# Fourier mixer on folded time with half the transform, its panels first; the products of the state-space tables one step behind their transposes

## The reference

```
ff = f.reshape(1, 1024, 4 heads, 64)
mixed = fft2(ff, axes=(time, channel of the head), norm='ortho').real
y_fft = einsum('bshd,hde->bshe', mixed, w_fft)
```

## Time and profile before

| | us |
|---|---|
| three runs | 2754.02, 2754.80, 2760.42 |
| median | 2754.8 |
| span of the profiled execution, first to last instruction | 2751.9 |
| median less that span | 2.9 |
| PE busy | 2637.7 |
| DVE, POOL, ACT busy | 1465.6, 1091.4, 1029.3 |
| mean granted clock of TensorE | 0.986 |

### The profile page before, as it was taken

How to read it: one execution, slowest core, us unless ns; L and a number is a source line. 1 busy time by engine, 2 the same in 40 slices (tenths; PEclk the granted TensorE clock), 3 DMA queues, 4 the chain that set the end, 5 groups by cost and what they waited for, 6 DMA issues and landing times.

```text
span 2751.9 us, 31627 instructions
## 1 busy us (share of the span) xinstructions
PE 2637.7 (96%) x12542; PEld 2080.4 (76%) x12542; DVE 1465.6 (53%) x1881; ACT 1029.3 (37%) x1600; POOL 1091.4 (40%) x605
## 2 busy tenths in 40 slices
PE   6889989999999999999999999999999999999997
PEld 2657757777888788877777788888788788888885
DVE  5646658797777722276766422433457655322225
ACT  4413655455444511345454321211354434312112
POOL 1322114256656544442211142322353655534443
PEclk8999999999999999999999999999999999999998
DMA  6453247321222343241123122111324233433322
GB/s 247 178 146 101 78 173 285 113 81 66 81 84 83 112 146 126 84 145 59 54 68 109 54 88 67 58 48 48 137 91 153 77 115 104 149 118 128 115 77 85
DMA packets 109619, 297.92 MB, mean 108 GB/s; under 512 B 13344, under 2 KB 28192, under 8 KB 109472
## 3 DMA queue, kind: packets, MB, share of 16 engines
q1 hardware_dynamic: 102592, 275.36, 29.4%
q10 hardware_dynamic: 3456, 10.73, 1.0%
q0 software_dynamic: 3424, 9.81, 0.9%
HBM read 233.09 MB, written 62.76 MB: 108 GB/s over the span
## 4 chain that ended last, share of the span: by engine, by line
PE 71%; DVE 5%; ACT 1%; issue 1%; POOL 1%; DMA 1%; POOLq 0%; SPq 0%; DVEq 0%; ACTq 0%
PE ps L1698 16%; PE ps L1700 15%; PE ps L1699 15%; PE ps L1732 5%; PE ps L1734 5%; PE ps L1733 5%; PE pc L1732 1%; PE pc L1734 1%; PE pc L1733 1%; PE pss L2026 1%; PE pc L2078 1%; PE pc L2080 1%; PE pc L2079 1%; POOL whl L3448 1%; DVE pad L2104 0%
## 5 line engine op out<-in xcount | busy, mean ns | idle before, releaser
L3448 POOL TENSOR_TENSOR whl<-wraw,whl 128x1024 fp32r<-128x1024 f32 (+2 forms) x309 | 648.0, 2102 | 1242.0 <-ACT whl L2918 1241.8
L1698 PE MATMUL ps<-act,whl 128*128 128x512 f32 x1824 | 735.5, 403 | 34.7 <-DVE act L2098 9.2
L1699 PE MATMUL ps<-act,whl 128*128 128x512 f32 x1824 | 718.0, 394 | 0.0
L1700 PE MATMUL ps<-act,whl 128*128 128x512 f32 x1824 | 717.5, 393 | 0.0
L1698 PEld LDWEIGHTS ps<-act,whl 128*128 128x128 f32 x1824 | 344.9, 189 | 134.9 <-issue 43.3
L2918 ACT ACTIVATE whl<-wraw 128x1024 fp32r<-128x1024 f32 (+2 forms) x309 | 268.1, 869 | 461.9 <-PE ps L1700 372.6
L1700 PEld LDWEIGHTS ps<-act,whl 128*128 128x128 f32 x1824 | 344.9, 189 | 76.9
L1699 PEld LDWEIGHTS ps<-act,whl 128*128 128x128 f32 x1824 | 345.3, 189 | 75.7 <-issue 4.1
L2098 DVE TENSOR_TENSOR y<-y,ps 128x512 f32<-128x512 f32 x176 | 120.9, 687 | 365.6 <-PE ps L1700 365.4
L1698 PE MATMUL ps<-hid,whl 128*128 128x512 f32 x544 | 216.8, 399 | 4.4 <-DVE y L2502 4.3
L1700 PE MATMUL ps<-hid,whl 128*128 128x512 f32 x544 | 214.4, 394 | 0.0
(11 more groups left out here) (402 smaller groups left out, 4206.1 us busy)
## 6 DMA issues: line engine op xcount, KB each, us to landing
wraw<-in_w_in SPq DMA_DIRECT2D x63, 512.0 KB, 3.4
wraw<-in_f1u SPq DMA_DIRECT2D x72, 256.0 KB, 2.8
wraw<-in_f2d SPq DMA_DIRECT2D x36, 512.0 KB, 3.4
wraw<-in_w_out SPq DMA_DIRECT2D x32, 512.0 KB, 3.4
x<-in_w_ada SPq DMA_DIRECT2D x32, 512.0 KB, 7.2
hid<-hscr SPq DMA_DIRECT2D x29, 512.0 KB, 6.6
xs<-y SPq DMA_DIRECT2D x24, 512.0 KB, 6.3
wraw<-in_f2u SPq DMA_DIRECT2D x48, 256.0 KB, 3.3
```

The lines of the kernel that those rows point to most:

```text
L1698: pe.matmul(PSB[g.bank][:, :], hi, x_hi, start=e == 0, stop=False)
L1699: pe.matmul(PSB[g.bank][:, :], hi, x_lo, start=False, stop=False)
L1700: m = pe.matmul(PSB[g.bank][:, :], lo, x_hi, start=False, stop=e == len(ks) - 1)
L3448: return g_.tensor_tensor(out, a, b, op)
```

## The change

Time is folded: for t = 1 to 511, e(t) = f(t) + f(1024-t) goes to a new tile `fe` and f(t) - f(1024-t) stays in fT (`fft_eo` on DVE); the cosine half needs e alone, the sine half the difference alone. So `fft_c` and `fft_s` run over 4 time tiles in place of 8; f(512) is carried separately (`fft_n`, two products of one column) and added with alternating sign in `fft_out`. All four `dft` panels are loaded once. Panels 8 and 9 come first in w_in; `fft_w` goes behind panel 1 on a bank half of `pss`, the stage behind panel 2. In `tables`, `tab_ko` moves from the step of its `tab_k` one or two steps on, and the thread has one step more.

```diff
-W_IN_ORDER = (0, 1, 2, 8, 9, 6, 7, 3, 4, 5)
+W_IN_ORDER = (8, 9, 0, 1, 2, 6, 7, 3, 4, 5)
...
-        def made_k(b0):
+        def turn_k(b0):
             p.put("tab_k", b0)
             p.put("tab_wst", b0)
+
+        def made_k(b0):
             p.put("tab_ko", b0)
             p.put("tab_kst", b0)
...
             if n:
-                made_k(b0 - GB)
+                turn_k(b0 - GB)
             yield
             p.put("tab_w", b0)
+            if n > 5:
+                made_k(b0 - GB)
             yield
             if n < 6:
                 p.put("tab_cs", n)
                 p.put("tab_cst", n)
+                if n:
+                    made_k(b0 - GB)
                 yield
+        turn_k(NG - GB)
+        yield
         made_k(NG - GB)
...
     def fourier():
-        p.put("fft_w", p.hold[0])
-        for tp in range(8):
-            p.pe(0.9, "fft_c", tp, p.hold[1])
+        for tp in range(4):
+            p.pe(0.9, "fft_c", tp, p.hold[0], p.hold[1])
             p.poll()
-        for tp in range(8):
+        p.pe(0.5, "fft_n")
+        for tp in range(4):
             p.pe(3.4, "fft_s", tp, p.hold[2], p.hold[3])
             p.poll()
-        p.pe(3.4, "fft_mid")
+        p.pe(1.8, "fft_mid")
...
-                if r[0] == 0:
-                    p.put("fft_load")
-            if r[0] == 9:
-                fourier()
+                if r[0] == 1:
+                    p.pe(1.8, "fft_w")
+                elif r[0] == 2:
+                    fourier()
+            if r[0] == 8:
+                p.put("fft_load")
+            if r[0] in (8, 9):
+                p.put("fft_eo", r[0] - 8)
...
                 if b < 5:
                     w.wait_ge(*done("ssmD", "rot", b + 1))
+                else:
+                    w.wait_ge(*done("ssmA", "y", 4))
...
                 for pr in range(2):
-                    w.wait_ge(*z_done(8 + pr))
-                    m = pe.matmul(PSB[tp % 2][:, pr * 256:pr * 256 + 256], fT[:, pr, tp * 128:tp * 128 + 128],
-                                  WC[:, pr, :, :].rearrange("p a b -> p (a b)"), start=True, stop=True)
+                    w.wait_ge(*done("fftD", "eo", pr))
+                    for i, part in enumerate((fe, fT)):
+                        q = pr * 256 + i * 128
+                        m = pe.matmul(PSB[tp % 2][:, q:q + 128], part[:, pr, c], WC[:, pr, i, :], start=True, stop=True)
...
+            def fft_n():
+                for pr in range(2):
+                    m = pe.matmul(PSS[:, 0, 2 + pr:3 + pr], WC[:, pr, 0, :], fT[:, pr, 512:513], start=True, stop=True)
...
                     for pr in range(2):
                         m = pe.matmul(PSB[2 * i + pr][:, :], FA[tp][:, pr, i * 128:i * 128 + 128],
-                                      dft[tp % 4][:, i * 512:i * 512 + 512], start=tp == 0, stop=tp == 7)
+                                      dft[tp][:, i * 512:i * 512 + 512], start=tp == 0, stop=tp == 3)
...
+            def fft_eo(pr):
+                f, back, e = fT[:, pr, 1:512], fT[:, pr, 1023:512:-1], fe[:, pr, :]
+                w.wait_ge(*z_done(8 + pr))
+                v.tensor_copy(e[:, 0:1], fT[:, pr, 0:1]).then_inc(*step("fftD"))
+                tt(e[:, 1:512], f, back, ALU.add).then_inc(*step("fftD"))
+                w.wait_ge(*last("fftD"))
+                tt(f, f, back, ALU.subtract).then_inc(*mark("fftD", "eo", pr))
...
-                v.tensor_copy(st[:, 0:512], Pb[:, :]).then_inc(*mark("fftD", "a", pr))
+                ts(st[:, 0:512:2], Pb[:, 0:512:2], n512, ALU.add).then_inc(*step("fftD"))
+                ts(st[:, 1:512:2], Pb[:, 1:512:2], n512, ALU.subtract).then_inc(*mark("fftD", "a", pr))
...
-            def load_d(tp):
-                if tp < 8:
-                    if tp >= 4:
-                        w.wait_ge(*done("fft", "s", tp - 4))
-                    q.dma_start(dft[tp % 4], t["dft"][tp]).then_inc(*dmark(f"d_q{tp % 4}", tp))
-
...
                 for tp in range(4):
-                    load_d(tp)
+                    q.dma_start(dft[tp], t["dft"][tp]).then_inc(*dmark(f"d_q{tp}", tp))
```

More of the change, by code:

```diff
@@ L1287, in build @@
         dist = sb("dist", [P, 384], c=pu)
-        alt = sb("alt", [P, 1], c=pu)
+        alt = sb("alt", [P, 3], c=pu)
         cp.close()
@@ L1299, in build @@
         FA6 = sb("FA", [P, 6, 2, 256], c=cf)
-        FA = [FA6[:, n, :, :] for n in range(6)]
-        FA += [uT[:, 0, 4 * n:4 * n + 4, :].rearrange("p t k -> p (t k)").rearrange("p (a b) -> p a b", a=2) for n in range(2)]
+        FA = [FA6[:, n, :, :] for n in range(4)]
+        fe = FA6[:, 4:6, :, :].rearrange("p n a b -> p n (a b)")
         cf.close()
@@ L1913, in att_out, with fft_w @@
                             m.then_inc(*mark("att", "o", u, g))
-            def fft_w(hold):
+            def fft_w():
                 w.wait_ge(*done("d_fw", "wf"))
-                w.wait_ge(*done(*hold))
+                w.wait_ge(*done("apD", "t", 0, 1, 7))
                 for pr in range(2):
@@ L1950, in fft_mid @@
                 w.wait_ge(*done("d_alt"))
-                w.wait_ge(*done("apD", "t", 0, 1, 7))
                 for pr in range(2):
-                    for tp in range(8):
-                        m = pe.matmul(PSS[:, 0, pr:pr + 1], FA[tp][:, pr, 0:128], alt[:, :], start=tp == 0, stop=tp == 7)
+                    for tp in range(4):
+                        m = pe.matmul(PSS[:, 0, pr:pr + 1], FA[tp][:, pr, 0:128], alt[:, 0:1], start=tp == 0, stop=tp == 3)
                 m.then_inc(*mark("fft", "mid"))
@@ L2084, in tensor @@
                      "tab_ko": tab_ko, "ssm_x": ssm_x, "ssm_y": ssm_y, "glu": glu, "att_v": att_v, "att_score": att_score,
-                     "att_t": att_t, "att_out": att_out, "fft_w": fft_w, "fft_c": fft_c, "fft_s": fft_s, "fft_mid": fft_mid,
+                     "att_t": att_t, "att_out": att_out, "fft_w": fft_w, "fft_c": fft_c, "fft_n": fft_n, "fft_s": fft_s, "fft_mid": fft_mid,
                      "r_rows": r_rows, "r_bc": r_bc, "r_rows2": r_rows2, "r_bc2": r_bc2, "lru_ri": lru_ri, "pool": pool, "hg_v": hg_v,
@@ L2408, in att_split, with fft_w, fft_n, fft_c @@
                     *mark("attD", "o", i, half))
-            def fft_w(hold):
-                w.wait_ge(*done("fft", "w"))
-                v.tensor_copy(WC.rearrange("p a b c -> p (a b c)"), PSB[0][:, :]).then_inc(*mark("fftD", "wc"))
-            def fft_c(tp, hold):
+            def fft_eo(pr):
[5 more added lines that the diff above has]
+                tt(f, f, back, ALU.subtract).then_inc(*mark("fftD", "eo", pr))
+            def fft_w():
+                w.wait_ge(*done("fft", "w"))
+                v.tensor_copy(WC.rearrange("p a b c -> p (a b c)"), PSS[:, 0, :]).then_inc(*mark("fftD", "wc"))
+            def fft_n():
+                w.wait_ge(*done("fft", "n"))
+                v.tensor_copy(alt[:, 1:3], PSS[:, 0, 2:4]).then_inc(*mark("fftD", "n"))
+            def fft_c(tp, *hold):
                 if tp % 2 == 0:
                     w.wait_ge(*done("fft", "c", tp))
-                    if tp == 6:
-                        w.wait_ge(*done("d_us0"))
                     v.tensor_copy(FA[tp].rearrange("p a b -> p (a b)"), PSB[0][:, :]).then_inc(
@@ L2432, in fft_out @@
                 w.wait_ge(*done("fft", "mid"))
-                v.tensor_copy(st[:, 512:513], PSS[:, 0, pr:pr + 1]).then_inc(*mark("fftD", "st", pr))
+                tt(st[:, 512:513], PSS[:, 0, pr:pr + 1], n512, ALU.add).then_inc(*mark("fftD", "st", pr))
             def fft_split(pr):
@@ L2895, in vector @@
                      "ssm_rot": ssm_rot, "ssm_scan": ssm_scan, "ssm_back": ssm_back, "glu_out": glu_out,
-                     "att_score": att_score, "att_norm": att_norm, "att_split": att_split, "fft_w": fft_w, "fft_c": fft_c,
+                     "att_score": att_score, "att_norm": att_norm, "att_split": att_split, "fft_eo": fft_eo, "fft_w": fft_w, "fft_n": fft_n, "fft_c": fft_c,
                      "fft_out": fft_out, "fft_split": fft_split, "nsum": nsum, "r_fac": r_fac, "r_add": r_add, "r_sum": r_sum, "r_fac2": r_fac2,
@@ L2984, in ev @@
                     if 3 <= g.i < 8:
-                        w.wait_ge(*done("fft", "s", 7))
+                        w.wait_ge(*done("fft", "s", 3))
                     if g.i < 3:
@@ L3173, in fft_c @@
                     w.wait_ge(*done("fft", "c", tp))
-                    if tp == 7:
-                        w.wait_ge(*done("d_us0"))
                     av(FA[tp].rearrange("p a b -> p (a b)"), PSB[1][:, :], ACT.Copy).then_inc(*mark("fftA", tp))
@@ L3741, in fft_load @@
                 for tp in range(4):
-                    load_d(tp)
-            def fft_s(tp, *hold):
-                load_d(tp + 4)
+                    q.dma_start(dft[tp], t["dft"][tp]).then_inc(*dmark(f"d_q{tp}", tp))
             def x_again(s):
@@ L3896, in _constants @@
     c, s = np.cos(ang), -np.sin(ang)
-    d = np.empty((8, 128, 1024), f)
-    for tp in range(8):
+    d = np.empty((4, 128, 1024), f)
+    for tp in range(4):
```

27 lines of the change are left out of this document (15 added, 12 removed).

## The result

| | kernel before | changed kernel |
|---|---|---|
| median of the runs on one chip, us | 2758.9 (7 runs) | 2766.9 (7 runs) |
| ratio, 95% interval | | 1.0032 (1.0021 to 1.0042) |
| span of the profiled execution, us | 2751.9 | 2764.2 |
| mean granted clock of TensorE | 0.986 | 0.979 |

The account below looks back on a forecast made before the run. PE was taken as the bound, busy 2637.7 of 2751.9 us: 34.3 us freed, but `ssm_x` 0 only 19.1 earlier, less 1.8 for half clock, called 17.5. Span 2734.4, median 2737, range 2724 to 2748.

Parts of the forecast that it names:

- the text's own signs: Observations listed beforehand as showing the forecast right or wrong, such as `ssm_x` 0 at 187 or later than 195.
- The stage itself: Fourier stage: halved second-stage products free 14.4 us of PE, `fft_mid` 2.0; strided PSUM reads in `fft_out` take 0.42 each.
- The 10.2 at L1801 go: Tables: PE's 10.2 us of waits for ACT copies vanish, since `tab_ko` comes a step or two behind its transposes.
- `fft_w` now lies a panel earlier on a bank of its own: 1.9: Fourier stage: the wait behind `fft_w` (0.9) and short waits in `fft_c` (1.0) go, freeing 1.9 us of PE.
- `ssm_x` 0 stands 24.5 us behind it: First SSM product: planned 36 k-steps behind the tile after the Fourier stage, so at 186.9, 19.1 us earlier, not 34.
- The last stretch 27: SSM end, last `ssm_x` to last product: 27 us in place of 37.8, counted as -11, since attention ends first.
- From there the chain is the old one, 16.5 us: Behind the last SSM product: copy, two DMA round trips, then gelu 16.5 us behind the product, as before.
- Everything behind glu is the same: Rest of the program behind glu: unchanged, following as one block with the 17.5 us gain.
- (A): PE is the only bound: the SSM keeps up and all 34.3 us arrive, less 1.8 or less; 2720 to 2722; 15%.
- (B): Table thread slips as `tab_v` waits for the later `tab_ko`: `ssm_x` 0 8 to 16 us later, 2746 to 2754; 12%.
- (C): ACT's strict queue gates the tables in each of eight batches, up to 45 us against 10: 2772, slower; 6%.
- the text's own bounds for the SSM stretches: SSM: three blocks at 35 us and a last stretch of 33 leave 0.5 us gain; two blocks at 18.7 give 28.

Follow-up runs that it names:

- e2: Changed kernel with the copy of the table product put ahead of the sines on ACT; 2757.6 us, ratio 1.0007 to the kernel before.
- e4: Kernel before with only the tables' part of the change (`tab_ko` moved later), no fold, old panel order; 2748.6 us, ratio 0.9977.
- e17: Changed kernel with the fold steps behind panels 0 and 1 and the weight product directly ahead of the Fourier stage; 2759.4 us, ratio 1.0014.
- e16: Kernel before with the tables' part, panels 8 and 9 first and the Fourier stage behind panel 2, unfolded; 2747.0 us, ratio 0.9966.
- e9: e2 with the table thread's planned distance cut from 2.6 to 2.0 us; 2750.5 us, ratio 0.9973 to the kernel before.
- e10: e9 with the first SSM product planned 7 us after its load instead of 14; 2732.2 us, ratio 0.9909 to the kernel before.
- e1: Changed kernel with the modulation step held back until gelu is issued; 2766.0 us, ratio 1.0040 to the kernel before.
- e7: Changed kernel with the whole modulation step held back until behind the fourth gate product; 2774.8 us, ratio 1.0064 to the kernel before.

## Why the prediction was wrong, step by step

The forecast span was 2734.4 and the measured one 2764.2, 29.8 us more. Of these, 18.2 were there at `ssm_x` 0 (205.1 for 186.9), 24.8 at the last product (373.8 for 349) and 34.3 at gelu (399.8 for 365.5); the rest of the program gave back 4.5. Three of the text's own signs came: `ssm_x` 0 later than 195, an idle of PE over 5 us at a `tab_k` (5.6), and a gap to gelu that was not 16 to 17.

**The stage itself was right.** There are 32 half-passes of 512 columns, and 22.2 us for 41.7, where the terms of the sum give 21.9 (41.7 less 14.4, 2.0 and the 3.4 of table products that move behind it). The strided reads of PSUM took 0.88 us for two (168.91), 0.44 each: the 0.42 taken, not the 0.69 of the upper bound. The Trainium skill (SBUF — State Buffer, "Door 1: The DMA port swizzle") says of matmuls that PSUM access which is not contiguous slows them; these are reads by DVE, and no slowdown shows in this row.

**"The 10.2 at L1801 go"** failed. By the terms of the sum the first `fft_s` product was due at 137.1 (155.0 less 17.9); it came at 152.1, and nearly all of the delay at E arises ahead of it. From 60 us up to it PE idled 16.8 us before (95.0 less 78.2 busy) and 16.9 now (92.1 less 75.2). The waits moved from `tab_ko` to the next transposes and are 8.8 us. I had taken a wait as gone since its product comes later, and not asked what stands between that product's copy on ACT and whoever needs it: the sines of the step before. e2 prices it at 7 to 9 us. e4 shows the term as I meant it: no such wait above 1.4 us and the `fft_s` products 10 us earlier than before.

**"`fft_w` now lies a panel earlier on a bank of its own: 1.9"** was booked as a gain only. Its copy is a wait at the head of DVE's queue, in the middle of a table batch; e17 puts that at 5 us. What stands behind that copy on DVE, the text did not ask. For `fft_eo` it did, and DVE was through it at 102.0, where the text had 101. But the batch behind it ended at 114.7 and not at 110: two of its ops took 5.32 us where the text counts 0.56 each. Against e16 the fold steps cost PE 2.4 to 3.5 us, so most of their 11 us were indeed covered. With these terms and PE at half clock behind the waits, the tile behind the stage came at 174.3 and not 159.0.

**"`ssm_x` 0 stands 24.5 us behind it"**: the mechanism was right, and is the main finding. With the 3.4 us of table products the text had 27.9; the distance was 30.8. PE waited for nothing in it (30.8 busy of 30.8): it ran 37 k-steps where the text had 36, and the passes behind E's wait at half clock (0.63 for 0.40), with a granted clock of 0.94 over the whole. With E late as well, the 19.1 us became 0.9. The forecast took the planner's distances as given and saw that 15 of the 34 us would be lost to them; e9 and e10 show those 15 and more.

**"The last stretch 27"**: 33.7 (340.03 to 373.77), near the bound of 33 that the text had kept. The cause was not in the text: attention ends first, so the splits and the w_out k-steps behind it fall into the last block, ahead of `ssm_y` 4 and so of the load that the last product waits for. The four blocks beside attention took what was said, 28 to 34 us.

**"From there the chain is the old one, 16.5 us"**: 26.0. I had named this as what would fell the forecast. The chain on the data's side is the old one (e10: 17.8), but what comes first on ACT and DVE changed when the SSM thread became the last to end: the modulation starts beside the end of attention and overtakes gelu. e1 has 19.5 us; 2 of the 3 us that are left over 16.5 are the last product's own passes, at half clock behind its wait (its four parts start 1.3 to 1.4 us apart where before they start 0.67 apart). e1 and e7 show that the gate then stands between two needs of the same DVE rows, and neither order gets the time back.

**"Everything behind glu is the same"** held, to 2 us.

**The rivals.** (A) fell: PE is the bound only once the SSM thread is not, and even in e10 the gain is 24 us of 34. (B) fell in its form: `tab_v` waited for PE once, 3.6 us at 161.2, with the stage already running. Its outcome, `ssm_x` 0 late by 8 to 16 us, was near to what came (18.2), by another way. (C) had the right engine and the right reason, a strict queue on ACT, and a price several times too high: 35 us, where e2 gives 7 to 9. As all or nothing it got 6%; no case held a cost of that kind of a quarter of the size, and that alone takes about half of the forecast gain. And the range ended at 2748, although the text's own bounds for the SSM stretches left a gain of 0.5.

**Left open:** what the fold's DVE steps cost in the changed kernel's own place (e16 prices them in e17's), what the fold is worth in the new planning with the panel order held fixed, and whether e10's 17.8 us between the last product and gelu can be shortened.

## What to carry to other kernels

Time that is taken out of one thread of an order written ahead of time is worth something only if the thread that ends last moves too: after shortening a stage, re-plan the threads that were spaced to fit it, and make the control with the new spacing and without the change. For a step that is moved, go through each in-order queue that it issues on and ask what its first wait now stands in front of; a wait that disappears at one instruction can turn up one instruction further, as here. And when two threads swap which ends last, whatever starts behind one of them or behind both (here the splits and the modulation) changes its place too.

## What the runs showed of the hardware that was not expected

DVE ops of one kind and size take very different times in the stretch around 100 us: two of 128x384 took 1.03 us in most places and 5.32 at 103.59, and the fold's subtract 2.73 at 99.30 against 0.69 for its twin at 95.82; e4's DVE has single ops of 2.6 us there as well, without the fold. POOL's splits (its rows are in the section on the SSM products) lie over just these: they end at 101.48, 105.84 and 108.49, DVE's stretched ones at 102.03 and 108.91. That is what the Trainium skill states (SBUF — State Buffer, "Who interferes with whom"): a VectorE op with two SBUF inputs and a GpSimd op that reads SBUF lock each other out for a whole instruction, and the later one waits. The trace agrees: DVE's stretched ops end 0.4 and 0.6 us behind a split. No run took the splits away. In the changed kernel the second batch lost 4.3 us so, and its third 2.2 (3.22 for 1.03 at 122.96); in e4 four ops of the second batch and its phases lost 2 us each. In the kernel before, DVE idled for its 11.54 us while these splits ran, so its ops met none of them; one op of its next batch took 2.64 us (at 125.76) beside a split.

And the time given back to PE is not all kept: the changed kernel granted 0.68 of the full clock over the 46.4 us ahead of the gate, and the gate's first 24 passes took 13.3 us, where twelve before took 5.3, 10.6 for as many. Most of that evens out within the gate, since before it was the last twelve that ran at half clock (7.11) and now they take 5.7: all 36 passes took 17.8 us before and 19.0 now.
